# Two attentions as one sequence, rotary sums beside the first attention, and two GEMMs begun with the rows that are ready

## What is computed

```python
h = _rms_norm(x, norm_mix_pre[l])
proj = h @ w_in[l]                    # dq, dk, dv, mq, mk, mv, c_q, c_kv, k_pe, g
oa = _diff_attention(...)             # 4 heads: softmax(q1 k1 + bias) - lam * softmax(q2 k2 + bias), times v
oa = _rms_norm(oa, diff_subln[l]) * (1.0 - lam_init)
ob = _moba_attention(...)             # 4 heads of 128; with 256 tokens: causal attention with a bias
q = _rms_norm(c_q, mla_q_norm[l]) @ mla_w_uq[l]       # 8 heads of 64 + 32, the 32 turned by _rope
kv = _rms_norm(c_kv, mla_kv_norm[l]) @ mla_w_ukv[l]   # and one rotated key for all heads
oc = _dense_causal_attention(q, k, kv[..., 64:], 1.0 / math.sqrt(96))
br = einsum('bsgc,gcd->bsgd', stack([oa, ob, oc]), w_branch[l])
mixed = sum(sigmoid(g) * br, axis=2) @ w_out[l]
x = x + _rms_norm(mixed, norm_mix_post[l])
h = _rms_norm(x, norm_mlp_pre[l])
x = x + _rms_norm(square(relu(h @ w_up[l])) @ w_down[l], norm_mlp_post[l])
```

## Time and profile before

| | |
|---|---|
| median of 3 runs | 3072.14 us |
| lowest and highest | 3069.19 and 3078.15 us |
| time of the profiled execution | 3069.35 us |
| its span, first to last instruction | 3067.5 us |
| mean granted TensorE clock | 0.987 |
| PE busy | 2976.7 us (97%) |
| DVE busy | 1822.4 us (59%) |
| ACT busy | 1175.9 us (38%) |
| DMA, mean | 137 GB/s |

### The profile page before, as it was taken

The page is one execution under the profiler, slowest core; times in us unless marked ns, Lnnn a source line. Parts: engine busy times, 40 slices in busy tenths (PEclk is TensorE's granted clock), DMA queues, the critical chain, the costliest instruction groups (busy, mean ns, idle before and its releaser), DMA issues. The chain is left out here.

```text
span 3067.5 us, 46310 instructions
## 1 busy us (share of the span) xinstructions
PE 2976.7 (97%) x19019; PEld 2647.2 (86%) x19019; DVE 1822.4 (59%) x3378; ACT 1175.9 (38%) x2019; POOL 166.7 (5%) x199
## 2 busy tenths in 40 slices
PE   7999999999999999999999998999999999999998
PEld 4888889888888888888888778999898999899998
DVE  4777775443569886743334445556656656656665
ACT  4222224333342222332223344444544544455453
POOL 2000010000010000100001110000002001001100
PEclk9999999999999999999999999999999999999999
DMA  7556552222236565632324324656335554435452
GB/s 231 151 165 185 158 163 92 73 69 83 69 95 186 185 195 175 194 88 84 110 71 126 92 78 111 186 167 191 97 118 185 165 185 137 138 97 172 152 185 91
DMA packets 509004, 421.42 MB, mean 137 GB/s; under 512 B 18235, under 2 KB 505963, under 8 KB 508793
## 3 DMA queue, kind: packets, MB, share of 16 engines
q1 hardware_dynamic: 505752, 412.33, 43.8%
q0 software_dynamic: 3040, 6.13, 0.8%
HBM read 417.30 MB, written 1.12 MB: 136 GB/s over the span
## 5 line engine op out<-in xcount | busy, mean ns | idle before, releaser
L1478 DVE TENSOR_TENSOR w_low<-raw,w_high 128x1024 fp32r<-128x1024 f32 (+2 forms) x720 | 765.3, 1104 | 321.0 <-ACT w_high L1004 319.8
L1004 ACT ACTIVATE w_high<-raw 128x1024 fp32r<-128x1024 f32 (+2 forms) x720 | 648.6, 950 | 648.6 <-PE gemm L2168 308.1
L2168 PE MATMUL gemm<-xh,w_high 128*128 128x512 f32 (+1 forms) x1904 | 688.4, 362 | 5.1 <-DVE xl L1516 4.5
L2168 PE MATMUL gemm<-xl,w_high 128*128 128x512 f32 (+1 forms) x1904 | 680.9, 358 | 0.0
L2168 PE MATMUL gemm<-xh,w_low 128*128 128x512 f32 (+1 forms) x1904 | 680.8, 358 | 0.0
L2168 PEld LDWEIGHTS gemm<-xh,w_high 128*128 128x128 f32 x1904 | 359.7, 189 | 62.0 <-issue 5.6
L2168 PEld LDWEIGHTS gemm<-xh,w_low 128*128 128x128 f32 x1904 | 359.2, 189 | 57.3
L2168 PEld LDWEIGHTS gemm<-xl,w_high 128*128 128x128 f32 x1904 | 359.6, 189 | 55.5 <-issue 0.2
L2168 PE MATMUL gemm<-yh,w_high 128*128 128x256 f32 x1216 | 350.7, 288 | 12.8 <-DVE yl L1541 7.1
L2168 PE MATMUL gemm<-yl,w_high 128*128 128x256 f32 x1216 | 345.5, 284 | 0.0
L2168 PE MATMUL gemm<-yh,w_low 128*128 128x256 f32 x1216 | 344.9, 284 | 0.0
(11 more groups left out here) (335 smaller groups left out, 4230.1 us busy)
## 6 DMA issues: line engine op xcount, KB each, us to landing
raw<-in_ffn_w_in SPq DMA_DIRECT2D x176, 512.0 KB, 5.2
raw<-in_w_mod SPq DMA_DIRECT2D x72, 1024.0 KB, 7.6
raw<-in_w_in SPq DMA_DIRECT2D x50, 1024.0 KB, 5.3
raw<-in_w_up SPq DMA_DIRECT2D x32, 1024.0 KB, 5.4
raw<-in_w_down SPq DMA_DIRECT2D x32, 1024.0 KB, 5.0
raw<-in_ffn_w_out SPq DMA_DIRECT2D x32, 768.0 KB, 4.6
raw<-in_ret_w_in SPq DMA_DIRECT2D x24, 1024.0 KB, 5.2
raw<-in_ffn_w_out SPq DMA_DIRECT2D x32, 640.0 KB, 4.0
```

What stands on the lines that cost most here:

```text
L1004: act.activation(wh[i % SPL][:, a:b], raw[slot_of["w", i]][:, a:b], ACT.Copy).then_inc(w_high, 1)
L1478: dve.tensor_tensor(wl[slot][:, a:b], raw[slot][:, a:b], wh[i % SPL][:, a:b].bitcast(F32), ALU.subtract).then_inc(w_low, 1)
L2168: ins = pe.matmul(out, l_, r_, start=first and j == 0, stop=last and j == 2)
```

## The change

Six edits, here by place in the program:

1. `nat`: four steps of `nat_o` follow attention steps 28, 29, 30 and 32 on PE: rows 0 to 4 of the first group, the same of the second, row 5 of both, row 6 of both. Row 7 is left for the end. A row waits for its own pair of outputs.
2. The eight sums of the rotary queries go, on DVE, one behind each of the first eight steps of `diff`; PE waits for them only before the scores of `mla`, ACT before it overwrites `yt`.
3. `diff`: min(8, 1 + x // 2) chunks after step x. The chunks stand behind the even steps in place of the odd ones, beginning after step 0.
4. `moba` and `mla` are one sequence of 12 pairs with 28 chunks beside it, min(28, x + 1 + x // 6) after step x. The waits for `o_low` and `sub_low` go to the chunks of branch 1 and branch 0 that read them.
5. `mixed`: six rows of the first group, then six of the second, each group waiting for its own weights and banks, then rows 6 and 7 of both.
6. `tail`: the squares come after 8 rows in place of 6 and the spreading after 14 in place of 10 where the half has two chunks; after 14 and 16 where it has four (`ret_out3`).

```diff
-        def alongside(name, steps, rest, lag=0):
-            a = atts[name]
+        def alongside(names, steps, rest):
             done = 0
-            for x in range(2 * len(a.pairs) + 1):
+            for x in range(2 * sum(len(atts[name].pairs) for name in names) + 1):
                 next(steps)
-                upto = {"nat": min(24, x - x // 13), "dif": (x + 1) // 2, "mob": min(4, 1 + (x + 1) // 2),
-                        "mla": x + (x + 1) // 2}[a.kind]
-                while done < upto - lag:
-                    next(rest)
+                upto = {"nat": min(24, x - x // 13) + (x >= 28) + (x >= 29) + (x >= 30) + (x >= 32), "dif": min(8, 1 + x // 2),
+                        "mob": min(28, x + 1 + x // 6)}[names[0][:3]]
+                while done < upto:
+                    next(rest, None)
                     done += 1
...
-                dve.wait_ge(roped_part, 4 * l + 2 * g + 2)
-                for j in range(4):
-                    q = slice(32 * j, 32 * j + 32)
-                    dve.tensor_tensor(mq[R, 4 * g + j, :], yt[q, g, :], yt[q, 2 + g, :], ALU.add).then_inc(roped, 1)
+            def with_sums(steps, l):
+                dve.wait_ge(roped_part, 4 * l + 4)
+                hd = 0
+                for _ in steps:
+                    if hd < MH:
+                        g, q = hd // 4, slice(32 * (hd % 4), 32 * (hd % 4) + 32)
+                        dve.tensor_tensor(mq[R, hd, :], yt[q, g, :], yt[q, 2 + g, :], ALU.add).then_inc(roped, 1)
+                    hd += 1
+                    yield 1
...
-                                    if hf_ and done == 6:
+                                    if hf_ and done == 3 * nt + 2:
                                         added_squares(N, 0)
...
-                                    if hf_ and done == 10:
+                                    if hf_ and done == (14 if nt == 2 else 16):
                                         spread(N, 0)
...
+                    for some, r0, r1 in ahead:
+                        for gi in some:
+                            bl, ch = pair[gi]
+                            pe.wait_ge(w_low, 2 * (s + gi) + 2)
+                            for ci in range(len(ch)):
+                                wait_chunk_out(pe, n + 2 * gi + ci - 4)
+                                for k in range(r0, r1):
+                                    if k not in seen:
+                                        x_waits(k)
+                                        seen.add(k)
+                                    products(n + 2 * gi, s + gi, 0, bl, ch, ci, k)
+                        yield 1
...
-                    for k in range(nk):
+                    for k in range(ahead[-1][2] if ahead else 0, nk):
...
+                    if a.kind == "mla" and p == 0:
+                        pe.wait_ge(roped, (MH + 1) * (a.layer + 1))
+                        pe.wait_ge(kpe_copied, (MH - 1) * (a.layer + 1))
...
-            pe.wait_ge(o_low, atts["nat"].p1)
-            run(gemm("nat_o"))
+            last = gemm("nat_o", lambda kc: pe.wait_ge(o_low, 2 * kc + 2), wide=True,
+                        ahead=(((0,), 0, 5), ((1,), 0, 5), ((0, 1), 5, 6), ((0, 1), 6, 7)))
...
-                pe.wait_ge(roped, (MH + 1) * (l + 1))
+                pe.wait_ge(roped, (MH + 1) * l + 1)
+                pe.wait_ge(roped_part, 4 * (l + 1))
...
-                alongside(f"moba{l}", behind_subln(attention(f"moba{l}")), gate)
-                pe.wait_ge(kpe_copied, (MH - 1) * (l + 1))
-                pe.wait_ge(sub_low, DH * (l + 1))
-                pe.wait_ge(o_low, atts[f"moba{l}"].p1)
-                alongside(f"mla{l}", attention(f"mla{l}"), both(*(gemm(o, by_chunk=True) for o in with_mla(l))))
+                names = f"moba{l}", f"mla{l}"
+                inputs = {f"branch0{l}": lambda kc: pe.wait_ge(sub_low, DH * (l + 1)), f"gate1{l}": None,
+                          f"branch1{l}": lambda kc: pe.wait_ge(o_low, atts[f"moba{l}"].p1)}
+                alongside(names, behind_subln(attention(*names)),
+                          both(gate, *(gemm(o, inputs[o], by_chunk=True) for o in with_mla(l))))
...
-                run(gemm(f"mixed{l}", lambda kc: pe.wait_ge(mix_low, 8 * l + kc + 1), wide=True))
+                run(gemm(f"mixed{l}", lambda kc: pe.wait_ge(mix_low, 8 * l + kc + 1), wide=True,
+                         ahead=(((0, 1), 0, DC - 2),)))
```

More of the change, by code:

```diff
@@ L574, in add_att @@
             a.nat = a.kind == "nat"
+            a.layer = 0 if a.nat else int(name[-1])
             a.apart = a.kind in ("nat", "dif")
@@ L792, in alongside, with pairs_of @@
             run(rest)
+        def pairs_of(names):
+            return [(atts[name], p) for name in names for p in range(len(atts[name].pairs))]
         def after_each(steps, parts):
@@ L1360, in _ @@
             run(gemm("nat_v0"))
-            alongside("nat", attention("nat"), both(*(gemm(f"nat_{k}{g}", by_chunk=True) for g in range(1, 4) for k in "qkv")))
+            alongside(("nat",), attention("nat"), both(*(gemm(f"nat_{k}{g}", by_chunk=True) for g in range(1, 4) for k in "qkv")))
             run(gemm("nat_o"))
@@ L1755, in attention @@
                     yield 1
-                out_low(n - 1)
+                out_low(*pairs[n - 1])
             def take_columns(q):
@@ L2024, in _ @@
                 run(steps)
-                alongside(f"diff{l}", attention(f"diff{l}"), both(*(gemm(o, by_chunk=True) for o in with_diff(l))), 0)
+                alongside((f"diff{l}",), with_sums(attention(f"diff{l}"), l), both(*(gemm(o, by_chunk=True) for o in with_diff(l))))
                 gate = gemm(f"gate0{l}", by_chunk=True)
@@ L2044, in _ @@
                                              op1=ALU.subtract).then_inc(sub_low, 1)
-                alongside(f"moba{l}", attention(f"moba{l}"), gate, 0)
-                alongside(f"mla{l}", attention(f"mla{l}"), both(*(gemm(o, by_chunk=True) for o in with_mla(l))), 0)
+                names = f"moba{l}", f"mla{l}"
+                alongside(names, attention(*names), both(gate, *(gemm(o, by_chunk=True) for o in with_mla(l))))
                 for q in range(4):
@@ L2296, in normed, with attention, scores @@
                 return lambda kc: pe.wait_ge(x_low, N["p0"] + per * (kc + 1))
-            def attention(name):
-                a = atts[name]
-                n = len(a.pairs)
+            def attention(*names):
+                pairs = pairs_of(names)
+                n = len(pairs)
                 rev, rev64 = cst[:, C_REV:C_REV + P], cst[:, C_REV64:C_REV64 + P]
-                order = {"nat": rev64, "dif": rev, "mob": rev, "mla": ident}[a.kind]
-                def scores(p):
+                def scores(a, p):
                     g, t = a.p0 + p, a.pairs[p]
-                    if a.apart or p == 0:
+                    order = {"nat": rev64, "dif": rev, "mob": rev, "mla": ident}[a.kind]
+                    if a.apart or a.kind == "mob" and p == 0:
                         if g:
@@ L2376, in values @@
                     ins.then_inc(o_ready, 1)
-                scores(0)
+                scores(*pairs[0])
                 yield 1
-                for p in range(n):
-                    if p + 1 < n:
-                        scores(p + 1)
-                    if p:
-                        values(p - 1)
-                    turn(p, 0)
+                for j, (a, p) in enumerate(pairs):
+                    if j + 1 < n:
+                        scores(*pairs[j + 1])
+                    if j:
+                        values(*pairs[j - 1])
+                    turn(a, p, 0)
                     yield 1
-                    turn(p, 1)
+                    turn(a, p, 1)
                     yield 1
-                values(n - 1)
+                values(*pairs[n - 1])
             pe.wait_ge(consts_in, 16)
@@ L2521, in _ @@
             run(gemm("nat_v0"))
-            alongside("nat", attention("nat"), both(*(gemm(f"nat_{k}{g}", by_chunk=True) for g in range(1, 4) for k in "qkv")))
-            pe.wait_ge(o_low, atts["nat"].p1)
-            run(gemm("nat_o"))
+            last = gemm("nat_o", lambda kc: pe.wait_ge(o_low, 2 * kc + 2), wide=True,
+                        ahead=(((0,), 0, 5), ((1,), 0, 5), ((0, 1), 5, 6), ((0, 1), 6, 7)))
+            alongside(("nat",), attention("nat"),
+                      both(*(gemm(f"nat_{k}{g}", by_chunk=True) for g in range(1, 4) for k in "qkv"), last))
             ffn(1, 1, 2)
```

81 lines of the change are left out of this document (41 added, 40 removed).

## The result

The changed kernel took **3057.6 us** (median of 4, 3057.5 to 3059.5), the kernel before 3074.2 on the same chip (3069.2 to 3078.2): a ratio of 0.9948, 95% interval 0.9931 to 0.9965. The prediction was 3057.0.

What follows compares the result with a forecast made beforehand. PE bounds the kernel (busy 2976.7 of 3067.5 us), so only its idle time and lower-clock matmuls can be won. Terms -10.2, -2.5, -0.7, +3.2, -4.9 sum to -15.1: median 3072.14 to 3057.0, range 3051 to 3063 (3044 to 3067 with two rivals).

Steps and rivals of the forecast that it cites:

- `mixed`, -10.2: Start of `mixed`: first group starts alone, so the 3.4 us wait and 1.7 of clock fall go, each layer.
- `nat`, -2.5: End of `nat`: three waits for ACT's copies (0.8, 0.7, 1.0 us) covered by early matmuls; no clock gain.
- The tails, -0.7: `ret_out3`'s tail: wait for squares moves to the next GEMM, at most a 1.7 us fall won; other three tails 0.
- `diff`, +3.2: `diff`: new waits for DVE's division, 8.4 us a layer against 5.1, less 1.7 of clock in each layer.
- the split's chain: `diff`, even pairs: division waits behind chunk copy and weight split, which hangs on ACT; 1.1 us for pair 2.
- 2 x 1.7: `diff`, both layers: clock expected to hold because idle time is spread, giving back 1.7 us a layer.
- `moba` and `mla`, -4.9: `moba` and `mla`: waits 2.7 us against 4.3 a layer, -3.2 in all, and layer 1's clock fall, -1.7.
- Sum, -15.1: Whole kernel: all terms together, giving 3052.4 us against the profiled span and 3057.0 against the median.
- the chunks cover `diff` after all: Rival in `diff`: divisions late only for the last pair, -9.0 in place of +3.2, 3044.8 us; chance 0.12.
- the clock is not given back: Rival: the struck clock falls return elsewhere, +8.5, 3065.5 us; chance 0.16.
- all five falls that were struck: Clock falls of 1.7 us each expected to go: `mixed` and `diff` in both layers, `moba`/`mla` in layer 1.
- Many short waits: Rival in `diff`: about eight 1 us waits a layer keep the clock down, 13 falls, 3082 us; chance 0.05.

Runs made afterwards that it cites:

- the second trace: The kernel before, unchanged, measured and profiled once more: 3074.5 us, ratio 1.0004.
- The kernel with the chunks between the turnings: Against the changed kernel, each further chunk of `diff` put between the two turnings of a pair, the first still after the first step: 3051.1 us.

## Why the prediction was right

**`mixed`, -10.2.** The step held: no wait, no fall, -10.2 in the two stretches.

**`nat`, -2.5.** The step that failed. "All longer than the wait" was right for the three waits (0.84, 0.75 and 1.02 us, not "a few tenths"), but it asked only what the early rows cover, not what they had covered where they were taken from. They were the cover of DVE's split and copy; the step should have gone on to the next thing that PE needs, a bank. In place of the three waits came one of 3.36 us and a fall that costs 1.7. The stretch came out +2.2 against the first trace and +1.1 against the second; by the times of the kernels without the edit it is a gain of 1.0 to 3.0.

**The tails, -0.7.** Size off: -2.4 in the trace. The wait moved as said; PE is 1.4 us less busy in this tail, inside the 1.7 that was the most expected of the clock, and twice the 0.7 that was taken; two of the other tails, taken at 0, gave 0.9, and no wait in the view says why.

**`diff`, +3.2.** Near the sum (+0.6 and +2.9), by two errors that cancel. The mechanism is as described, and undone by putting a chunk back ahead of each turning. The waits were put too high: for odd pairs 0.7 was said and 0.35 to 0.40 came, since PE is 1.36 us behind the end of the chunk and not 1.1, and the division done at 1.65 and not 1.8; for pairs 2, 4 and 6 it was 1.1, 0.8 and 0.8 against 0.71, 0.51 and 0.50, with the split's chain as described and a few tenths shorter. And the clock was not given back as 2 x 1.7. In layer 0 the fall behind the wait for exponentials did go:

```profile
2164.27 1.08 PE L2320 MATMUL aux<-diff_qk_gate 64*128 64x256 f32 x4 [2.96 <-ACT pexp L1187]
2164.50:2167.90 3.40, 3.40 (x12) 2.39 (x11) 1.50 (x4) 0.61 (x3) 0.00 (x0) 0.50 0.02 5
```

(before), but PE's busy time over the stretch fell by 0.4 us only. After, in both layers:

```profile
2149.49:2212.00 62.51, 56.39 (x436) 51.30 (x436) 40.30 (x83) 27.91 (x71) 4.68 (x7) 1.00 0.33 102
2630.52:2695.08 64.56, 58.08 (x438) 53.00 (x438) 40.31 (x83) 28.16 (x71) 4.68 (x7) 0.97 0.32 98
```

Before, it was 56.81 of 61.86 and 56.93 of 61.63 us at 0.97. The kernel with the chunks between the turnings, also without a fall, is busy for 55.6 us in layer 0, 1.2 less than before and 0.8 less than after. Most of that 0.8 can come from the waits themselves: a chunk's matmul is recorded as 0.28 us long and the next starts 0.12 us after it, so each wait lets the last one run on alone for 0.16 us (estimate: with four waits more than in that kernel 0.6 us). In layer 1 the clock fell again, behind the last waits, at 2688.5. The gain, too, was put down to the wrong edit: "the 3.0 us for the exponentials of pair 0 is covered by the new chunk" is true, but the sums alone would have taken most of it.

Three rows show DVE's order at work: the copy at 1874.95 right behind the split in `nat_o`, the division at 2171.27 behind the copy of the chunk, the maxima at 2163.09 behind sums and split. That agrees with the strict queue of ScalarE and VectorE in the Trainium skill ("TensorE: Matmul & The Clock Gate", section "Architectural detail: the array is 16× 32×32, not 1× 128×128").

**`moba` and `mla`, -4.9.** Measured -2.3 and -3.4, together -5.7; the waits left are 3.1 us a layer, 2.7 was said. So the waits gave less than forecast, 1.2 in layer 0, and some 1 us a layer came beside them, from PE's busy time, which the sum had at nothing and no run explains.

**Sum, -15.1.** The spans differ by 9.9 against the first trace of before and 17.2 against the second, the medians by 16.6. The first trace was one of the fastest executions of its kernel. That the prediction also set its sum against the median was what saved it, and that the total came within 0.6 us is in part luck: `nat` alone was off by 3.6 to 4.7 us, and the tails, `moba` and `mla`, and the choice of the median stood against it.

**The rivals.** That the chunks cover `diff` after all fell for this order and holds for the one with the chunks between the turnings. That the clock is not given back is true in part: all five falls that were struck stayed away, but two new ones came, at 1876 and 2688.5, and three times 1.7 is the 5.2 us by which PE's busy time fell. (The 6.8 us at 1.2 GHz from 2861 on are there after as well, in two parts, at 2852 and 2869.) Many short waits did not hold the clock down: 6.1 us of waits in layer 0 of `diff` left it at 1.00.

## What to carry to other kernels

Work that is begun early to cover one wait is taken away from where it stood; follow the engine that releases the next buffer (here DVE, with a weight split in front of a copy) before counting the gain. In an in-order queue beside PE, move an item that has slack out from in front of the one that PE waits for; where it can't be moved, leave work on PE between the two: one such move of each kind, of a split on DVE and ACT and of the chunks on PE, gave 12 us more on top of the 16.6 of the whole change. And before an edit is credited with a wait, ask whether another edit of the same change removes it too.

## What the runs showed of the hardware

Two executions of the same program had PE's waits at the same places and differed by 7 us through the clock alone (0.987 and 0.985). Behind the four waits of 2.96 to 3.41 us it fell each time, in both traces of the kernel before; behind the waits of about 1 us between `moba` and `mla` in layer 0 it fell in the second trace (at 2250) and not in the first. So a difference of 2 to 3 us between single traces of two kernels shows nothing unless a wait goes with it, and the removal of a wait can be worth more than the wait and its own fall (16.5 us for 6.8 of waits in `mixed`) or less (4.9), depending on what the clock does elsewhere.
